# Moving a third of the first stage's scaling from VectorE to GpSimd in a hybrid decoder step

## The reference

```python
sh1, sc1, gt1, sh2, sc2, gt2 = ada_mod(c, w_ada, b_ada)      # silu(c) @ w_ada + b_ada
h = rms_norm(x, rms_g1) * (1 + sc1) + sh1
q, k, v, hc, bgate, cgate, ga, gb = project_in(h, w_in, q_norm_g, k_norm_g)
o_att = attend(q, k, v, sb_bias)                              # stick-breaking attention
yc, conv_state = short_conv(cgate * hc, conv_prev, conv_w, conv_b)
x = x + gt1 * merge_branches(o_att, bgate * yc, ga, gb, w_att_out, w_conv_out, w_o)
h2 = rms_norm(x, rms_g2) * (1 + sc2) + sh2
x = x + gt2 * sqrelu_mlp(h2, w_mlp1, w_mlp2)
```

## Time and profile before

| | us |
|---|---|
| median of 3 runs | 1663.25 |
| lowest, highest | 1662.4, 1663.83 |
| the profiled execution, whole | 1661.66 |
| its span, first to last instruction | 1659.8 |
| TensorE busy | 1612.9 (97% of the span) |
| VectorE busy | 960.8 (58%) |
| GpSimd busy | 637.9 (38%) |
| ScalarE busy | 447.8 (27%) |

### The profile page before, as it was taken

One profiled execution on the slowest core, in us unless ns is written; L12 is line 12 of the kernel. 1 busy time (PEld: TensorE's weight loads), 2 busy tenths in 40 slices (PEclk: granted clock), 3 DMA queues, 4 the chain that ended last, 5 costly groups with the idle time before them and its releaser, 6 DMA issues.

```text
span 1659.8 us, 31738 instructions
## 1 busy us (share of the span) xinstructions
PE 1612.9 (97%) x12312; PEld 1499.2 (90%) x12312; DVE 960.8 (58%) x1630; ACT 447.8 (27%) x802; POOL 637.9 (38%) x440
## 2 busy tenths in 40 slices
PE   7999999999999999999999998999999999999998
PEld 5898788878778878799999988999999999999998
DVE  5554364564544454437753689766666666666666
ACT  6344222222222322232111452222222222222220
POOL 0345143333334333413343226444444444444440
PEclk9999999999999999999999999999999999999999
DMA  9113346666656666534421100111111111111112
GB/s 384 41 44 98 145 161 223 214 204 217 201 177 235 218 232 215 167 130 170 157 103 51 39 26 26 52 52 52 52 52 52 51 52 52 52 52 52 52 39 105
DMA packets 71942, 194.74 MB, mean 117 GB/s; under 512 B 8018, under 2 KB 8147, under 8 KB 71795
## 3 DMA queue, kind: packets, MB, share of 16 engines
q1 hardware_dynamic: 67394, 178.62, 31.9%
q10 hardware_dynamic: 4400, 14.10, 2.3%
HBM read 174.26 MB, written 18.42 MB: 116 GB/s over the span
## 4 chain that ended last, share of the span: by engine, by line
PE 88%; DVE 5%; issue 2%; ACT 2%; POOL 1%; DMA 1%; SPq 0%; ACTq 0%; DVEq 0%; POOLq 0%
PE psum L809 74%; PE psum L934 2%; PE psum L959 2%; PE psum L947 2%; PE psum L983 2%; PE psum L1007 2%; PE psum L839 1%; POOL wl L710 1%; DMA pre<-in_weights 1%; DVE h2L L1805 1%; DVE rsq L1857 1%; POOL wh L708 1%; DVE sc L1837 1%; DVE act L1555 1%; PE psum L859 0%
## 5 line engine op out<-in xcount | busy, mean ns | idle before, releaser
L792 POOL TENSOR_TENSOR wl<-raw,wh 128x512 fp32r<-128x512 f32 x148 | 211.3, 1432 | 325.3 <-ACT wh L1409 325.3
L809 PE MATMUL psum<-hH,wh 128*128 128x352 f32 x832 | 276.5, 332 | 1.3 <-POOL wl L710 0.8
L809 PE MATMUL psum<-hL,wh 128*128 128x352 f32 x832 | 267.6, 322 | 0.0
L809 PE MATMUL psum<-hH,wl 128*128 128x352 f32 x832 | 267.0, 321 | 0.0
L809 PE MATMUL psum<-hidH,wh 128*128 128x352 f32 x768 | 248.5, 324 | 5.4 <-DVE act L1924 5.4
L809 PE MATMUL psum<-hidH,wl 128*128 128x352 f32 x768 | 248.0, 323 | 0.0
L809 PE MATMUL psum<-hidL,wh 128*128 128x352 f32 x768 | 247.8, 323 | 0.0
L735 POOL TENSOR_TENSOR beta<-beta,kb 128x512 f32<-128x512 f32 (+3 forms) x96 | 122.6, 1297 | 288.4 <-DVE kb L1607 288.4
L809 PEld LDWEIGHTS psum<-hH,wh 128*128 128x128 f32 x832 | 156.1, 188 | 28.4 <-issue 25.6
L1924 DVE SCALAR_TENSOR_TENSOR act<-psum,mods,act 128x352 f32<-128x352 f32 x256 | 145.3, 579 | 49.7 <-PE psum L809 49.5
L809 PE MATMUL psum<-h2H,wh 128*128 128x264 f32 (+1 forms) x544 | 159.7, 294 | 4.2 <-POOL wl L788 4.2
(11 more groups left out here) (239 smaller groups left out, 3341.0 us busy)
## 6 DMA issues: line engine op xcount, KB each, us to landing
raw<-in_weights SPq DMA_DIRECT2D x152, 512.0 KB, 3.6
ring<-in_cache_k SPq DMA_DIRECT2D x128, 256.0 KB, 3.9
ring<-in_cache_v SPq DMA_DIRECT2D x128, 256.0 KB, 3.6
pre<-in_weights SPq DMA_DIRECT2D x16, 512.0 KB, 16.2
gate_scratch<-gt ACTq DMA_DIRECT2D x14, 528.0 KB, 3.3
act<-gate_scratch SPq DMA_DIRECT2D x14, 528.0 KB, 4.8
xt<-in_xT SPq DMA_DIRECT2D x8, 528.0 KB, 7.0
act<-in_xT SPq DMA_DIRECT2D x8, 528.0 KB, 4.8
```

Source lines behind the costliest of these rows:

```text
L792: pool.tensor_tensor(xl, source_of(i), x.bitcast(F32), ALU.subtract).then_inc(S["split"], 1)
L809: mm = pe.matmul(out, x, y, start=n == 0, stop=n == end)
```

## The change

GpSimd gets 16 instructions ahead of `split(2)`: for each feature block it multiplies `xt` of the last 320 columns by `rst`, waits for itself, and multiplies the product by the block's scale, a column broadcast over 320 elements. Both work in place. It waits for the same `mods_done` as VectorE does, and signals a new semaphore, `scaled_rest`. VectorE scales the first 704 columns alone: 8 instructions of 320 columns leave it. ScalarE's `first_hi` waits for `scaled` for the 704 columns and for `scaled_rest` for the 320.

```diff
+            pool.wait_ge(S["rstd"], NCH)
+            for b in range(DB):
+                pool.wait_ge(S["mods_done"], 2 * b + 1)
+                cols = first_cols[1]
+                mark(pool.tensor_tensor(xt[:, b, cols], xt[:, b, cols], rst[:, cols], ALU.mult))
+                pool.wait_ge(S["pool_step"], steps[0])
+                pool.tensor_tensor(xt[:, b, cols], xt[:, b, cols], mods[:, DB + b, 0:1].to_broadcast([P, LASTP]), ALU.mult)\
+                    .then_inc(S["scaled_rest"], 1)
             for u in range(2, 8):
                 split(u)
...
             def first_hi(b, x):
                 cols = first_cols[x]
-                act.wait_ge(S["scaled"], 2 * b + x + 1)
+                act.wait_ge(S["scaled_rest"] if x else S["scaled"], b + 1)
                 act.activation(hH[:, b, cols], xt[:, b, cols], ACT.Identity, bias=mods[:, b, 0:1]).then_inc(S["h_hi"], 1)
...
-            act.wait_ge(S["scaled"], 2 * DB + 1)
+            act.wait_ge(S["scaled"], DB + 1)
             act.activation(hH[:, :, samp], hs[:, :, :], ACT.Copy).then_inc(S["h_hi"], 1)
...
             for b in range(DB):
                 dve.wait_ge(S["mods_done"], 2 * b + 1)
-                for cols in first_cols:
-                    stt(xt[:, b, cols], xt[:, b, cols], mods[:, DB + b, 0:1], rst[:, cols], ALU.mult, ALU.mult)\
-                        .then_inc(S["scaled"], 1)
+                cols = first_cols[0]
+                stt(xt[:, b, cols], xt[:, b, cols], mods[:, DB + b, 0:1], rst[:, cols], ALU.mult, ALU.mult).then_inc(S["scaled"], 1)
                 first_lo(b)
```

More of the change, by code:

```diff
@@ L525, in program @@
             ada_in13 ada_in14 ada_in15 squares_added csig c_ready split_high gain_ready squares_in_acc ada_copied ada_turned conv_first squares rms_done rstd dense_done bank_dve bank_act dve_step act_step
-            ada_done mods_done scaled h_hi h_lo h_sample head_ready qk_sq qk_sq_hi qk_sq_lo qk_sum qk_rs qk_ready kout vout
+            ada_done mods_done scaled scaled_rest h_hi h_lo h_sample head_ready qk_sq qk_sq_hi qk_sq_lo qk_sum qk_rs qk_ready kout vout
             z_done beta_done scan_done a_done at_done at_out0 at_out1 av_done o_out
```

## The result

The changed kernel takes 1667.62 us (median of 9 runs, 1665.59 to 1669.59), the kernel before 1663.21 (9 runs, 1662.21 to 1664.43): ratio 1.0027, 95% interval 1.0017 to 1.0036, 4.4 us slower. The forecast was 1665.75 with a range to 1667.6: too low by 1.9 us, and the median lies just outside. The profiled run after took 1669.59 us (span 1667.8, mean granted TensorE clock 0.992) against 1661.66 (span 1659.8, 0.996) before.

The account below looks back on a forecast made before the run. TensorE's queue of matmuls was taken to bound the kernel. Losses of 0.5 us (blocks 0 and 2), 0.45 (block 3), 1.45 (blocks 4 to 7) and 0.1 make 2.5, added to 1663.25: 1665.75, range 1663.0 to 1667.6.

Parts of the forecast that it names:

- TensorE bounds, and the shift is rigid: Whole kernel: TensorE, busy 97% of the span, bounds; a shift of the dense groups' start at 54.52 shifts the end.
- The removal is worth nothing: VectorE losing 8 instructions of 320 columns, 3.7 us: all becomes waiting for `hH`; gain 0, at most 0.1 us.
- Durations of GpSimd: GpSimd's two added 320-column instructions per block: 0.87 us with two full inputs, 0.72 us with a broadcast input.
- VectorE and GpSimd exclude each other when both read two inputs: Block scaling: with two SBUF inputs each, the one starting first goes; GpSimd would hold the pair 0.73 and 0.58 us.
- The loop of VectorE: Blocks where GpSimd is first: VectorE's own loop bounds at 3.97 us a block instead of 3.61, 0.36 more.
- The price of one lost race: Block 0 or 2 with GpSimd first at a fresh start: 0.70 us lost each.
- Who goes first at a fresh block: Blocks 0 to 2: VectorE, 0.04 us ahead, goes first; GpSimd gets in first only from block 3.
- the second rival: GpSimd goes first in every block, if the pair is granted at the work's start: 3.3 us, 1666.6; chance 0.24.
- two lost 0.24 and one 0.45: Blocks 0 and 2 each lose 0.24 us with VectorE first; block 3, where GpSimd gets in, loses about 0.45 once.
- The rival's price: GpSimd first in every block: blocks 0 and 2 lose 0.70 each, the other five 0.36 to 0.4; 3.3 us, chance 0.24.
- the mixed forecast: VectorE first in blocks 0 to 2, GpSimd first from block 3: 2.5 us, 1665.75; chance 0.36.

Follow-up runs that it names:

- memset: Changed kernel with GpSimd's two multiplications per block replaced by two memsets of the same 320 columns, which read nothing: 1662.19 us, 0.9996 against the kernel before.
- before4: Fourth trace of the unaltered kernel before, one run: 1662.86 us, stage 33.54 us at a granted clock of 0.67.
- block0: Changed kernel with GpSimd scaling the 320 columns of block 0 alone, VectorE those of blocks 1 to 7: 1664.05 us, 1.0007 against the kernel before.
- tt: Changed kernel with the block's scale left out of VectorE's 704-column product, so it reads no column: 1663.3 us, 0.9999 against the kernel before.
- late: Changed kernel with GpSimd scaling the 320 columns of blocks 2 to 7 only, VectorE those of blocks 0 and 1: one run, 1665.47 us.
- mods2: Changed kernel with GpSimd waiting for the block's second modulation column, 0.16 us later: 1663.59 us, 1.0003 against the kernel before.
- one_rst: Changed kernel with only GpSimd's product with `rst` kept, the block's scale left out for the last 320 columns: one run, 1667.63 us.
- thirds: Kernel before, without GpSimd's work, its 704 columns per block handled as two chunks of 352, each released to TensorE by itself: 1661.01 us, 0.9986.
- before3: Third trace of the unaltered kernel before, one run: 1661.54 us, stage 32.48 us at a granted clock of 0.84.

## Why the prediction was wrong, point by point

- **TensorE bounds, and the shift is rigid**: right up to there: 558.9 to 559.1 us from the first dense matmul to the small matmuls ahead of the cache's in four traces of each kernel.
- **The removal is worth nothing**: right (memset: 0.9996 with 8 instructions gone; the stage 0.15 us shorter than *before4* at the same clock).
- **Durations of GpSimd**, 0.87 and 0.72 us interpolated: 0.86 to 0.88 and 0.72.
- **VectorE and GpSimd exclude each other when both read two inputs**: right, both ways, and with GpSimd only writing it is gone.
- **The loop of VectorE**, 3.97 us a block: 4.01. **The price of one lost race**, 0.70: 0.65 (block0).
- **Who goes first at a fresh block**: wrong, and this step decided the forecast. It took the order of the starts, which the earlier trace rows seemed to give, and VectorE was indeed 0.04 us ahead. But the starts do not decide: the runs fit a grant of the shared access when an instruction's work begins. VectorE's scaling with its column spends about 0.2 us ahead of its work, GpSimd 0.14, both estimates from durations. That was the condition of the second rival, worked out to ready times of 0.21 and 0.23, and given a chance of 0.24. (The prediction takes the scaling's own work as 0.73 us there and 0.75 elsewhere; the earlier trace rows give 0.74, from 0.952 less 0.546 for 384 columns, and the same order.) The earlier trace rows had no case that could tell: VectorE's instructions there read no column. tt shows it by turning the order round with starts as close as before, late and mods2 by a head start of 0.12 to 0.2 us, with which the instruction with the column wins. In place of the forecast's two lost 0.24 and one 0.45 the changed kernel lost the race in all eight blocks, and ran at 4.01 us a block from block 3 on.
- **The rival's price**, 3.3 us, was worked out from a trace with the clock at 0.84. At that clock one_rst, which has the same races and the same 4.01 us, is 35.95 - 32.46 = 3.5 us above the kernel before. At 0.67 on both sides it is 36.52 (mean of four) - 33.54 = 3.0. The rival was right in its order and within 0.3 in its size.
- **Left out of every case**: the clock and the rest of the kernel. The prediction expected no change of either. The four traces of the changed kernel stand at 36.52 - 32.46 = 4.1 us above the kernel before at 0.84, so 0.6 above the 3.5; and what lies behind the first dense matmul is 0.2, 0.3, 0.8 and, in the first trace, 3.6 us longer than the mean of the four before (1607.3), the last with the wait for the cache and the slow matmuls behind it. 4.1 and the middle of these, less what a slow stretch in one of four runs adds to the kernel before (0.3), is the measured 4.2 to 4.4. This sum was put together after the fact from few traces; the runs don't show that the change causes these two terms, so the last 1.0 us between the second rival's 1666.6 and the measured 1667.6 stays in part open.
- **The Trainium skill**, "SBUF — State Buffer", section "Who interferes with whom", says that issue order and not the shape of the operation decides who blocks. Taken to the letter it gave the mixed forecast. The traces disagree where the starts lie within 0.05 us: VectorE's instruction started first in the changed kernel and was blocked, and the shape (a column read or not) turned it. With starts 0.12 us or more apart they agree.

## What to carry to other kernels

Where both read two inputs, as here, work handed to GpSimd can cost VectorE's next step the time that GpSimd's first instruction holds the shared access, whatever the average load says; so first ask whether that step is in the bounding loop, and if it is, let GpSimd wait for a later signal so that it loses the race (here a start 0.2 us later took the loss from 4.4 us to 0.2, which is within the measurement; the stage itself is still 0.6 us longer). Where a race is decided by hundredths of a microsecond, forecast both orders and find a row with the very same operands before choosing one. And before moving work off an engine, see whether it is the load or the length of the way to the next engine that bounds: shortening that way (thirds) gained 2.4 us (0.8 to 4.0), and taking a third of the scaling off VectorE gained nothing.

## What was not expected of the hardware

- Which instruction starts first does not decide a close race. With VectorE 0.04 to 0.05 us ahead, the instruction with a column operand lost and took 1.65 us; the one without won and took 0.89.
- GpSimd's product with a broadcast column (320 columns) takes 0.72 us, with two full inputs 0.87, and it holds VectorE up by as much less.
- The same kernel in the same stretch is granted a mean clock of 0.84 or of 0.67 from one run to another (*before3* and *before4*), worth 1.1 us of stage. In one_rst the stretch from 53.4 to 63.4 us fell to 0.83 as well, behind a wait of 1.83 us; in the changed kernel a wait of 1.81 at the same place left it at 1.00.
```profile
53.40:63.40 10.00, 8.20 (x40) 7.82 (x41) 5.31 (x12) 3.44 (x7) 0.38 (x1) 0.83 0.00 1
```
